# Modulation slots four at a time, one column block per column tile, pairs written out

## The reference

```python
def adaln_params(c, w_ada, b_ada):
    m = jax.nn.silu(c) @ w_ada + b_ada                 # c: 9 sequences x 2048, w_ada: 2048 x 18432
    return jnp.split(m[:, None, :], 3 * N_SUBLAYERS, axis=-1)
...
    sh1, sc1, gt1, sh2, sc2, gt2, sh3, sc3, gt3 = adaln_params(c, w_ada, b_ada)
    x = x + MACARON * gt1 * swiglu(modulate(x, g_ffn1, sh1, sc1), w1_ffn1, w3_ffn1, w2_ffn1)
    heads, state = mixer(modulate(x, g_mix, sh2, sc2))
    x = x + gt2 * (heads @ w_out)
    x = x + MACARON * gt3 * swiglu(modulate(x, g_ffn2, sh3, sc3), w1_ffn2, w3_ffn2, w2_ffn2)
```

## Time and profile before

| | |
|---|---|
| median of 3 runs | 2674.47 us (2669.15 to 2677.79) |
| span of the profiled execution | 2673.7 us |
| TensorE busy | 2522.4 us, 94% |
| VectorE, ACT busy | 1159.7 us, 919.7 us |
| modulation matmuls L503 from adaw | 112.2 us busy, 1792 instructions |
| DMA | 230 GB/s mean |

### The profile page before, as it was taken

How to read it: one execution, slowest core, us unless ns; L and a number is a source line. 1 busy time by engine, 2 the same in 40 slices (tenths; PEclk the granted TensorE clock), 3 DMA queues, 4 the chain that set the end, 5 groups by cost and what they waited for, 6 DMA issues and landing times.

```text
span 2673.7 us, 53818 instructions
## 1 busy us (share of the span) xinstructions
PE 2522.4 (94%) x20995; PEld 2321.7 (87%) x20995; DVE 1159.7 (43%) x1767; ACT 919.7 (34%) x1155; POOL 44.6 (2%) x86
## 2 busy tenths in 40 slices
PE   6898999999999999899999777797999999999999
PEld 3597999999999999799997343597999999999999
DVE  0343444444444445666652111255444544454444
ACT  1432323233333334566541112245333333333332
POOL 0130000000000000000000000000000000000000
PEclk7798999999999999999999878898999999999999
DMA  8887777777767764344456999943444444454444
GB/s 355 341 313 230 286 267 286 275 283 267 289 219 281 277 230 162 128 157 150 164 210 256 389 361 408 349 161 125 161 168 165 165 165 165 159 171 165 165 159 159
DMA packets 105867, 614.13 MB, mean 230 GB/s; under 512 B 16192, under 2 KB 16464, under 8 KB 56128
## 3 DMA queue, kind: packets, MB, share of 16 engines
q1 hardware_dynamic: 101728, 603.81, 61.5%
q0 software_dynamic: 4064, 9.26, 1.3%
HBM read 604.36 MB, written 8.66 MB: 229 GB/s over the span
## 4 chain that ended last, share of the span: by engine, by line
PE 87%; DMA 8%; SPq 2%; DVE 1%; ACT 1%; issue 1%; ACTq 0%; DVEq 0%
PE banks L562 26%; PE banks L563 25%; PE banks L564 25%; PE banks L503 4%; DMA adax<-in_w_ada_dram 2%; PE banks L830 1%; PE banks L787 1%; DMA adaw<-in_w_ada_dram 1%; SPq L440 1%; DMA kv_raw<-in_vpool_dram 1%; PE banks L514 1%; DMA raw<-in_w_dram 1%; PE banks L649 1%; PE banks L661 0%; PE banks L773 0%
## 5 line engine op out<-in xcount | busy, mean ns | idle before, releaser
L562 PE MATMUL banks<-h_hi,w_hi 128*128 128x288 f32 x3792 | 1129.1, 298 | 28.6 <-DVE h_lo L1127 23.1
L563 PE MATMUL banks<-h_lo,w_hi 128*128 128x288 f32 x3792 | 1122.6, 296 | 0.0
L564 PE MATMUL banks<-h_hi,w_lo 128*128 128x288 f32 x3792 | 1121.2, 296 | 0.0
L1095 DVE TENSOR_TENSOR w_lo<-raw,w_hi 128x1024 fp32r<-128x1024 f32 (+2 forms) x666 | 763.8, 1188 | 378.7 <-ACT w_hi L867 372.4
L867 ACT ACTIVATE w_hi<-raw 128x1024 fp32r<-128x1024 f32 (+2 forms) x666 | 667.8, 1030 | 554.0 <-PE banks L564 507.3
L562 PEld LDWEIGHTS banks<-h_hi,w_hi 128*128 128x128 f32 x3792 | 717.0, 189 | 50.2 <-issue 43.7
L563 PEld LDWEIGHTS banks<-h_lo,w_hi 128*128 128x128 f32 x3792 | 716.9, 189 | 0.8
L564 PEld LDWEIGHTS banks<-h_hi,w_lo 128*128 128x128 f32 x3792 | 716.3, 189 | 0.0
L562 PE MATMUL banks<-g_hi,w_hi 128*128 128x288 f32 x1376 | 409.2, 297 | 0.0
L563 PE MATMUL banks<-g_lo,w_hi 128*128 128x288 f32 x1376 | 406.8, 296 | 0.0
L564 PE MATMUL banks<-g_hi,w_lo 128*128 128x288 f32 x1376 | 406.6, 296 | 0.0
(11 more groups left out here) (186 smaller groups left out, 1134.7 us busy)
## 6 DMA issues: line engine op xcount, KB each, us to landing
raw<-in_w_dram SPq DMA_DIRECT2D x172, 1024.0 KB, 4.8
adaw<-in_w_ada_dram SPq DMA_DIRECT2D x112, 1024.0 KB, 6.4
raw<-in_w_dram SPq DMA_DIRECT2D x64, 896.0 KB, 4.6
raw<-in_w_in_dram SPq DMA_DIRECT2D x49, 1024.0 KB, 4.8
adax<-in_w_ada_dram SPq DMA_DIRECT2D x32, 1024.0 KB, 8.3
raw<-in_w_dram SPq DMA_DIRECT2D x32, 960.0 KB, 4.7
raw<-in_w_out_dram SPq DMA_DIRECT2D x16, 1024.0 KB, 4.8
kv_raw<-in_kpool_dram SPq DMA_DIRECT2D x24, 512.0 KB, 6.0
```

Of the source, the lines that this page charges most:

```text
L562: pe.matmul(bank[:, 0:T], hi, m_hi[:, k, :], start=k == 0, stop=False)
L563: pe.matmul(bank[:, 0:T], hi, m_lo[:, k, :], start=False, stop=False)
L564: last = pe.matmul(bank[:, 0:T], lo, m_hi[:, k, :], start=False, stop=k == nk - 1)
L1095: dve.tensor_tensor(w_lo[:, r, a:b], raw[:, r, a:b], w_hi[:, r, a:b].bitcast(F32), ALU.subtract).then_inc(S["lo_ready"], 1)
```

## The change

Four slots are taken at once: four column blocks, the same half of the rows, one column tile for each block, so that each tile holds a whole sum over its half and, after a second batch with the other half, the block's result. Two batches make a unit of eight slots. One copy by ACT, two transposes by TensorE and one bias addition by VectorE end a unit. Batch t runs at the start of pair 2t, unit ends after tile A of every fourth pair from pair 2 on. Two more buffers, `adaw_b`, lie over `hf` and most of `sq`. Hence SP waits, ahead of the first batch, for `h_ready` 4 and `rev_stored`. The first body stands behind the first pair. The 56 pairs are written out in the program and not looped.

```diff
+        adaw_b = at("adaw_b", [P, 2, KT * P], F32, top[0] - 4 * SQL * T * 4)
+        adaq = [adaw[:, 0, :], adaw[:, 1, :], adaw_b[:, 0, :], adaw_b[:, 1, :]]
...
         def run(seg, eng, body, first=0, chain=None, per=0):
 
+            if seg.ada:
+                for i in range(first, seg.bodies):
+                    body(i)
+                return
...
+        UNITS = 8 + (ADA - 2 * KT) // 8
+        def ends_unit(seg, i):
+            return seg.ada and (seg.pair0 + i) % 4 == 2
+        def unit_of(seg, i):
+            return 8 + (seg.pair0 + i) // 4
...
-            def ada_pair(seg, i):
-                for j in range(2):
-                    if not (isinstance(i, int) and seg.pair0 + i == 0):
-                        sp.wait_ge(S["ada_used"], 2 * KT + 2 * seg.pair0 + j - 1 + 2 * i)
-                    sp.dma_start(adaw[:, j, :], w_ada[bass.ds(2 * KT + 2 * seg.pair0 + 2 * i + j, 1), :, :]
-                                 .rearrange("a p n -> p (a n)")).then_inc(S[f"ada_landed{j}"], 16)
+            def ada_batch(seg, i, part):
+                g = seg.pair0 + i
+                if g and g % 2 == 0:
+                    return
+                t = (g + 1) // 2
+                if t == (ADA - 2 * KT) // 4:
+                    return
+                if part == 0:
+                    sp.wait_ge(S["ada_used"], 2 * KT + t)
+                    if t == 0:
+                        sp.wait_ge(S["h_ready"], SQR)
+                        sp.wait_ge(S["rev_stored"], 16)
+                for j in (2 * part, 2 * part + 1):
+                    sp.dma_start(adaq[j], w_ada[2 * KT + 2 * (t // 2 * 4 + j) + t % 2, :, :])\
+                      .then_inc(S[f"ada_landed{j}"], 16)
 
             def stream(some):
                 for seg in some:
                     def body(i, seg=seg):
                         slot(seg, 0, i)
+                        if seg.ada and (i or seg.b0):
+                            ada_batch(seg, i, 0)
+                        slot(seg, 1, i)
+                        if seg.ada and not (i or seg.b0):
+                            ada_batch(seg, i, 0)
                         if seg.ada:
-                            ada_pair(seg, i)
-                        slot(seg, 1, i)
+                            ada_batch(seg, i, 1)
...
             def ada_body(seg, i):
+                g = seg.pair0 + i
+                t, half = g // 2, g // 2 % 2
+                if g % 2:
+                    return
+                if half == 0:
+                    pe.wait_ge(S["ada_sb"], unit_of(seg, i))
+                for j in range(4):
+                    pe.wait_ge(S[f"ada_landed{j}"], 16 * (t + 1))
+                for k in range(KT // 2):
+                    for j in range(4):
+                        last = pe.matmul(ada_part[32 * j:32 * j + 32, 0:2 * P], sc32[:, half * KT // 2 + k, :],
+                                         adaq[j][:, k * 2 * P:(k + 1) * 2 * P], start=half == 0 and k == 0,
+                                         stop=half == 1 and k == KT // 2 - 1, tile_position=(0, 32 * j))
+                last.then_inc(S["ada_used"], 1)
+            def ada_turn(u):
+                pe.wait_ge(S["ada_sb"], u + 1)
+                pe.wait_ge(S["ada_fin"], u)
+                for c in range(2):
+                    last = pe.transpose(ada_selp[:, c * P:(c + 1) * P], part_sb[:, c * P:(c + 1) * P], ident)
+                last.then_inc(S["ada_sel"], 1)
...
             def first_pair(seg, r):
-                if seg.ada:
-                    ada_body(seg, 0)
...
                 if seg.ada:
-                    ada_select(8 + seg.pair0, 2)
+                    ada_body(seg, 0)
...
-                if seg.ada:
-                    ada_copy(8 + seg.pair0 + i, 2)
+                if ends_unit(seg, i):
+                    ada_copy(unit_of(seg, i), 2)
...
-                if seg.ada:
-                    ada_finish(8 + seg.pair0 + i, 2 * KT + 2 * seg.pair0 + 2 * i, 2)
+                if ends_unit(seg, i):
+                    unit_finish(unit_of(seg, i))
```

More of the change, by code:

```diff
@@ L275, in decoder_layer @@
         names = """ld_small ld_x w_landed0 w_landed1 hi_ready lo_ready w_used acc_a_read acc_b_read ada_landed0
-            ada_landed1 adax_landed0 adax_landed1 adax_landed2 adax_landed3 ada_used ada_sb ada_sel ada_fin
+            ada_landed1 ada_landed2 ada_landed3 adax_landed0 adax_landed1 adax_landed2 adax_landed3 ada_used ada_sb ada_sel ada_fin
             c_ready sq_ready sq_used y0_ready hf_ready hhi_ready hn_ready gain_ready h_ready g_ready
@@ L302, in decoder_layer @@
         out = next(s for s in segs if s.kind == "down" and s.moving == "h")
-        PAIRS = 8 + (ADA - 2 * KT) // 2
+        UNITS = 8 + (ADA - 2 * KT) // 8
[3 more added lines that the diff above has]
+            return 8 + (seg.pair0 + i) // 4
         qk, vv = segs[segs.index(fa) - 1], segs[segs.index(fa) + 1]
@@ L589, in pair @@
                 tile(seg, 0, i, acc_a)
-                if seg.ada:
-                    ada_select(8 + seg.pair0 + i, 2)
+                if ends_unit(seg, i):
+                    ada_turn(unit_of(seg, i))
                 pe.wait_ge(S["acc_b_read"], seg.rb + i)
@@ L1152, in ada_finish, with unit_finish @@
                    .then_inc(S["ada_fin"], 1)
+            def unit_finish(u):
+                dve.wait_ge(S["ada_sel"], u + 1)
+                t0 = 2 * KT + 8 * (u - 8)
+                dve.tensor_tensor(par3[:, t0:t0 + 8, :].rearrange("p (j c) x -> p j c x", j=4),
+                                  ada_selp[:, 0:2 * P].rearrange("p (c j x) -> p j c x", c=2, j=4)[:, :, :, 0:NC],
+                                  ba[:, t0:t0 + 8].rearrange("p (j c) -> p j c", j=4).unsqueeze(3).to_broadcast([P, 4, 2, NC]),
+                                  ALU.add).then_inc(S["ada_fin"], 1)
             def gain(r, groups):
@@ L1219, in body @@
             def body(seg, i, late):
-                behind = (seg.norm is not None or seg is out) and isinstance(i, int)
+                behind = (seg.norm is not None or seg is out) and isinstance(i, int) and i == 0
                 if not behind:
@@ L1244, in segments @@
                     if seg.gate == 2 and seg.b0 == CHUNKS[0][1]:
-                        half_gate(2, 8 + 8)
+                        half_gate(2, 8 + 2)
                     if seg is ffn1[-1]:
-                        gain(1, PAIRS)
-                        gain(2, PAIRS)
-                        half_gate(8, PAIRS)
+                        gain(1, UNITS)
+                        gain(2, UNITS)
+                        half_gate(8, UNITS)
                     body(seg, 0, late)
```

## The result

| | before | after |
|---|---|---|
| median of 4 runs | 2675.56 us (2669.15 to 2677.79) | 2771.36 us (2768.85 to 2773.90) |
| ratio | | 1.0364, 95% interval 1.0349 to 1.0379 |
| span of the profiled execution | 2673.7 us | 2766.8 us |
| TensorE busy | 2522.4 us, 94% | 2482.3 us, 90% |

The change makes the kernel 3.6% slower. In the experiments, two executions at a much lower granted clock (4079.50 us of e10, 3136.74 us of the kernel before beside e5 to e8) are left out of the times and ratios. The page of the changed kernel: engine totals, then TensorE's and the DMA's rows of the 40 slices (69 us each), then the shares of the chain.

What follows compares the result with a forecast made beforehand. TensorE, 87% of the chain, was taken as the bound, with SP's new wait stalling it. Span 2673.7 + 135.6 (late pair 2) - 28.6 (later savings) - 13.9 (crowding) = 2766.8 us; forecast 2768 us, range 2742 to 2787.

Steps and rivals of the forecast that it cites:

- The landing of rev: GpSimd's store of rev, which SP awaits before batch 0: issued at 210.2, landing at 242, bounds 228 and 247.
- the lower bound of 228: Earliest landing of rev's store, at toe's rate of 1024 KB in 11.3 us, making 17 us for 1532 KB.
- From the landing to pair 2: Start of the kernel: batch 0 at 254.3, pair 2's tile A at 282.0 instead of 146.37, 135.6 us late.
- The wait at slot 3: TensorE waits 5.1 us (0 to 10) before tile B, as SP holds slot 3's load behind batch 1's wait.
- What is saved later: After pair 2: 26 batches at 3.79 us and 14 turns at 0.44 replace bodies and selects, saving 28.6 us.
- The crowding: 13.9 us lost from 207.19 to 266.73 beside rev's store in the kernel before; gone after the change.
- Written out pairs: Writing out the pairs and not looping them is worth zero, as in the win stage: 13.66 us either way.
- The fast loop: Rival: GpSimd's 64 loads run faster with SP silent, the store lands at 180, time 2706 us; chance 0.06.
- The early wait: Rival: store landed by 131, pair 2 only 25 us late, change faster at 2657 us; chance 0.04.
- Late tiles after the second batch: Rival: loads in fours make a weight tile late at every batch, 133 us more, 2900 us; chance 0.04.
- No overlap of the column tiles: Rival: column tiles don't overlap in the new order, some 10 us more per batch, above 3000 us; chance 0.01.
- The eight-engine rival: Rival: eight engines alone carry rev's store in 24.5 us, landing at 236, time 2762 us; chance 0.20.

Runs made afterwards that it cites:

- e10: Kernel before with the store of rev cut into eight, one per head after each 8 small loads; 2659.25 us, ratio 0.9922.
- e5: e6 with the store of rev put off until the last modulation unit is done; 2662.26 us, ratio 0.9938.
- e8: Changed kernel, wait kept, with the store reading eight rows of an input in DRAM and not rev; 2754.72 us, one run.
- e1: Changed kernel with rev moved out of adaw_b's bytes and SP's wait for rev_stored dropped; 2663.04 us, ratio 0.9936.
- e2: Kernel before with only SP's wait for h_ready 4 and rev_stored added ahead of slot 2; 2791.49 us, one run.
- e3: Kernel before with the 56 pairs written out and not looped, nothing else; 2672.98 us, ratio 0.9981.
- e4: Changed kernel, wait kept, with GpSimd issuing the store of rev before its 64 small loads; 2683.16 us, one run.
- e7: Kernel before with rev moved apart and its store issued only after the last modulation pair; 2677.24 us, ratio 0.9995.
- e6: e1 with slots 2 and 3 and two batch 0 loads ahead of the h_ready wait, slot 4 between batch 1's halves; 2662.28 us, 0.9937.
- e9: e6 with batch 1's four loads together and the store of rev cut into eight, one per head; 2659.32 us, ratio 0.9934.
- e12: Kernel before with rev stored once (12 KB), then its 128 copies per row made DRAM to DRAM; 2662.54 us, ratio 0.9949.

## Why the prediction was right, step by step

The forecast was 2768 us and 2766.8 of span; 2771.36 and 2766.8 were measured. The mechanism was the one named: e1 and e2 take it away and put it in alone. The span agrees to the decimal because small errors cancel, so look at the terms. (The profiled execution took 2768.85 us, the shortest of the four; that the median lies 2.5 us above it is most of the 3.4 us by which the forecast is off.)

**The landing of rev.** 242 was forecast, from the rate of the store's fastest stretch in the trace of before. It left 1.2 us earlier and took 33.8 us and not 31.5 (1.1 for the issue and 30.4): SP resumed at 242.80. Taking the same transfer's rate as the price, and not that of toe from the same array, was the choice that carried the forecast. toe reads from DRAM, and from there e8's store took 12.3 us: the lower bound of 228 belonged to a different kind of transfer.

**From the landing to pair 2.** Batch 0 began at 255.26 (254.3 forecast) and took 6.29 us (6): the granted clock stood at 0.50, the 1.2 GHz level, for most of it, where the trace of before has it after idling too. The wait at slot 3 was 5.8 us (5.1). One term was missing. In that wait the clock fell again, and tile B paid for it. Windows of the changed kernel (stretch, length, busy time of PE, PEld, DVE, ACT, POOL with instructions, granted clock, DMA share, GB/s):

```profile
256.00:258.00 2.00, 2.00 (x24) 1.11 (x20) 0.00 (x0) 0.38 (x1) 0.00 (x0) 0.50 0.39 160
...
268.00:270.00 2.00, 0.05 (x1) 0.00 (x0) 0.00 (x0) 0.00 (x0) 0.00 (x0) 1.00 1.01 426
...
274.00:276.00 2.00, 2.00 (x9) 2.00 (x10) 0.85 (x1) 0.00 (x0) 0.00 (x0) 0.50 1.01 426
276.00:278.00 2.00, 2.00 (x11) 2.00 (x11) 0.00 (x0) 0.00 (x0) 0.00 (x0) 0.59 1.01 422
278.00:280.00 2.00, 2.00 (x17) 2.00 (x16) 0.00 (x0) 0.00 (x0) 0.00 (x0) 1.00 0.99 385
```

The first row is of batch 0. The others are of slot 3's wait and of tile B: at 0.50 TensorE does 9 matmuls of 288 columns in 2 us, at 1.00 it does 17. Tile B took 8.3 us (273.87 to 282.15), not the 6.35 of the sum. Pair 2's tile A started at 285.74 and not 282.0: 3.7 us of error, half of it this one.

**What is saved later.** A batch costs (29.18 - 2 x 12.69) = 3.80 us; 3.79 was forecast. That the column tiles had run side by side before, so that one entry is all that a batch saves, holds. A turn costs 29.40 - 29.18 = 0.22 us, where 0.44 was taken and 0.2 was the lower bound: a turn adds to the pair only half of what two transposes showed in the earlier trace rows. 14 turns make the saving 3.1 us larger: 28.6 + 3.1 = 31.7, against the 31.71 of e2's comparison. (With the terms as written, the sum's 133.3 is 133.5, and the saving 0.2 us more.) The crowding was put at 13.9 and measured 13.90 in e2. These 3.1 us cancel most of the 3.7 above, and the stages after the square sum, 0.7 us shorter than before (1582.1 against 1582.7), the rest.

**Written out pairs**: zero was forecast. e3's interval puts the gain at 0.1 to 0.3%, 2 to 8 us, its two profiles at 0.1 us of span and 0.5 us of TensorE's stretch. Whether it is zero stays open; nothing in the sum needs more.

**The rivals.** The fast loop is refuted by the 1.51 us at 206.69 and 208.20. The early wait didn't occur; but its price can be read off e1, where the wait is absent: 2663, against the forecast 2657 for a wait met by 131, and the 7.7 us of crowding that e1 still has, and that rival's sum did not, are more than the difference. Late tiles after the second batch: TensorE's waits between 276 and 1190 hold none for a load or a split, only 1.3 us at the square sum. No overlap of the column tiles: refuted by the 3.59 us of 64 matmuls. The eight-engine rival gave 2762, from a store of 24.5 us, and it took 33.8. Its premise fared better than its price, and that belongs to the last section.

## What to carry to other kernels

A semaphore wait in a queue that loads everything costs what its latest event costs, for all that stands behind it: before reusing a buffer's bytes, look up when their last reader really ends in the trace, not in the program. Here e1 removed 108 us by giving a 12 KB array another address. And count the clock after each new stall: the wait of 5.8 us at slot 3 cost 1.9 us more in the tile behind it.

## What the runs showed of the hardware

**The store's pace comes from its source.** 1532 KB from 8 partitions took 33.8 us with no other traffic, 34.2 in e4 beside GpSimd's small loads alone, 33.9 in e5 and 34.0 in e7 beside weights in another stage, 34.4 (e6), 35.8 (e1) and 37.0 (before) beside weights and modulation loads. That is 46 GB/s alone and 42 at the slowest. The same bytes from DRAM took 12.3 us alone, 128 GB/s. That company makes a difference of only 10% was not expected; the prediction had put a lower bound 14 us below. Whether it is the 8 partitions as such or another property of that source was not tried: no run varies the number of partitions alone. The stores of e9 and e10 read one partition each and were slower still, 20 and 21 GB/s, but they are smaller and run beside loads, too; e10's:

```profile
rev_dram<-rev POOLq DMA_DIRECT2D x8, 191.5 KB, 9.1
```

**Half of the engines.** While the store runs alone, its queue holds 48.3% of the 16 engines' time, and 43.7% while e8's runs. The Trainium skill ("DMA: Bandwidth & Descriptors", section "Why a DMA increments its semaphore by 16 and not by 1") has a DMA spread over the largest number of engines up to 16 that divides the slowest dimension of both patterns; with 8 heads that is eight, and both shares agree with it. What it doesn't give is the duration, and there the rival went wrong: fewer engines said nothing of how long a packet lasts.

**A slow store in one piece costs others more than its bytes.** At 42 to 46 GB/s the store had TensorE wait 8 to 13 us in every place where it ran in one piece beside weights (before 12.8, e1 7.7, e6 12.1, e5 11.2, e7 13.0); at the 426 GB/s of the windows above its bytes would take 3.7 us. In e12, with the same bytes in 19.3 us, TensorE has no wait left between 150 and 300. In e10 the store is slower, in eight pieces; its queue, the small loads included, between 125 and 262:

```profile
q0 software_dynamic: 2436, 1.82, 28.2%
```

28.2% of 137 us is some three times the engine time of 34.0% of 36 us, and yet TensorE's only wait between 120 and 300 is 0.9 us, in the first pair. So the sum of the engine time isn't what it waits for; a stretch too long for the tiles loaded ahead fits these runs. That it is the occupied engines on which a weight load's share must queue is argued from the shares, not shown: no view here tells single engines apart.
